# Gate, up and router contract over features 8p+k instead of 128k+p

## The reference

```
x = layer_norm(ALPHA * x + gate1 * (y @ w_out))              # end of the first half
u = x * (1 + scale2) + shift2                                # [512, 1024]
logits  = u @ router_w + router_b                            # 16 experts
# softmax; one group of 4 experts is selected, then 2 experts in it; their scores are normalised
h   = silu(u @ w_gate[e]) * (u @ w_up[e])                    # w_gate, w_up: [16, 1024, 512]
out = sum over the two experts of score * (h @ w_down[e])    # w_down: [16, 512, 1024]
x = layer_norm(ALPHA * x + gate2 * out)
```

## Time and profile before

| | |
|---|---|
| median of 3 runs | 802.93 us (801.92 to 802.96) |
| time of the profiled execution | 803.91 us |
| span of the profiled execution | 802.1 us |
| TensorE matmul busy | 661.9 us, 83% |
| VectorE busy | 346.2 us, 43% |
| ScalarE busy | 249.6 us, 31% |
| GpSimd busy | 120.6 us, 15% |
| moved by DMA | 189.10 MB |
| mean granted TensorE clock | 0.914 of full speed |

### The profile page before, as it was taken

One profiled execution on the slowest core, in us unless ns is written; L12 is line 12 of the kernel. 1 busy time (PEld: TensorE's weight loads), 2 busy tenths in 40 slices (PEclk: granted clock), 3 DMA queues, 4 the chain that ended last, 5 costly groups with the idle time before them and its releaser, 6 DMA issues.

```text
span 802.1 us, 15163 instructions
## 1 busy us (share of the span) xinstructions
PE 661.9 (83%) x5977; PEld 433.7 (54%) x5978; DVE 346.2 (43%) x652; ACT 249.6 (31%) x514; POOL 120.6 (15%) x188
## 2 busy tenths in 40 slices
PE   0799999999897999999987297978997769999800
PEld 0376665777675777777866144534553334555400
DVE  0365553597787856856995500100110000111148
ACT  0344333766454554544012011111111111111144
POOL 0211000200000000000363121211221111222230
PEclk9999999999998999999995589998998798999955
DMA  9999865643112222138849969999999989982152
GB/s 302 373 282 342 273 230 179 222 119 104 55 52 80 80 79 78 57 118 301 339 136 345 349 222 400 400 344 378 330 348 328 378 324 393 335 317 78 42 214 105
DMA packets 109905, 189.10 MB, mean 236 GB/s; under 512 B 4904, under 2 KB 57352, under 8 KB 106800
## 3 DMA queue, kind: packets, MB, share of 16 engines
q1 hardware_dynamic: 96288, 149.05, 53.4%
q0 software_dynamic: 7136, 31.60, 11.0%
q10 hardware_dynamic: 6448, 8.00, 2.8%
HBM read 174.96 MB, written 13.67 MB: 235 GB/s over the span
## 4 chain that ended last, share of the span: by engine, by line
PE 53%; DVE 13%; SPq 13%; DMA 11%; ACT 6%; issue 4%; POOL 0%; DVEq 0%; ACTq 0%; POOLq 0%
PE psum L1431 11%; PE psum L1251 8%; SPq L380 8%; PE psum L1252 8%; PE psum L1253 8%; DMA wu<-in_moe_w_up_dram 7%; PE psum L1442 6%; SPq L385 3%; DMA raw<-in_w_in_dram 3%; PE psum L1217 2%; DVE u L1044 2%; PE psum L1294 1%; SPq L394 1%; PE psum L1306 1%; PE psum L1414 1%
## 5 line engine op out<-in xcount | busy, mean ns | idle before, releaser
L1431 PE MATMUL psum<-wg,xs 128*32 128x256 f32 x1280 | 159.1, 403 | 28.2 <-DMA wu<-in_moe_w_up_dram 24.9
L1431 PE MATMUL psum<-wu,xs 128*32 128x256 f32 x1280 | 158.9, 403 | 0.0
L1251 PE MATMUL psum<-uh,whi 128*128 128x512 f32 x336 | 138.2, 411 | 0.0
L1252 PE MATMUL psum<-ul,whi 128*128 128x512 f32 x336 | 131.7, 392 | 0.0
L1253 PE MATMUL psum<-uh,wlo 128*128 128x512 f32 x336 | 131.6, 392 | 0.0
L1431 PEld LDWEIGHTS psum<-wg,xs 128*32 128x32 f32 x1280 | 75.6, 115 | 84.1 <-DMA wu<-in_moe_w_up_dram 28.9
L1165 DVE TENSOR_TENSOR h_sb<-psum,hsil 64x256 f32<-64x256 f32 x40 | 17.1, 427 | 199.4 <-ACT hsil L759 199.4
L847 DVE TENSOR_TENSOR wlo<-raw,whi 128x1024 fp32r<-128x1024 f32 x42 | 51.4, 1224 | 64.1 <-ACT whi L605 63.9
L1442 PE MATMUL psum<-wd,hT 128*32 128x256 f32 x1280 | 78.2, 385 | 0.4 <-DVE hT L1169 0.4
L1431 PEld LDWEIGHTS psum<-wu,xs 128*32 128x32 f32 x1280 | 74.0, 115 | 3.4 <-issue 3.3
L1251 PEld LDWEIGHTS psum<-uh,whi 128*128 128x128 f32 x336 | 63.5, 189 | 20.5 <-issue 7.1
(11 more groups left out here) (253 smaller groups left out, 862.8 us busy)
## 6 DMA issues: line engine op xcount, KB each, us to landing
wg<-in_moe_w_gate_dram SPq DMA_DIRECT2D x32, 1024.0 KB, 12.3
wu<-in_moe_w_up_dram SPq DMA_DIRECT2D x32, 1024.0 KB, 17.1
wd<-in_moe_w_down_dram SPq DMA_DIRECT2D x32, 1024.0 KB, 14.6
raw<-in_w_in_dram SPq DMA_DIRECT2D x42, 512.0 KB, 4.0
ada<-in_ada_w_dram POOLq DMA_DIRECT2D x16, 1024.0 KB, 6.9
ada<-in_ada_w_dram SPq DMA_DIRECT2D x8, 1024.0 KB, 17.0
y_d<-ysb ACTq DMA_DIRECT2D x40, 128.0 KB
y_d<-zrow POOLq DMA_DIRECT2D x8, 512.0 KB, 6.3
```

The costliest lines, as they stand in the source:

```text
L1251: mmul(bank[s % 2], h[:, k, :], uh[:, k, :], start=(k == 0), stop=False)
L1252: mmul(bank[s % 2], h[:, k, :], ul[:, k, :], start=False, stop=False)
L1431: ins = mmul(psum[32 * g:32 * g + 32, 0, 0:256], xs[:, k % 2, k // 2, :], wgu[slot][g // 2][:, k, (g % 2) * 256:(g % 2) * 256 + 256], star ...
```

## The change

The gate, up and router weights are loaded with the view "(p k)" instead of "(k p)": partition p holds the features 8p to 8p+7, which are adjacent rows in DRAM. A half of k of the gate or up weights is then four adjacent rows of 2 KB on each partition. The down weights keep their order. To match, VectorE writes u2 in the order of (k, p): column 128k+p of a u2 tile holds feature 8p+k. It reads `zt`, `a2r` and `b2r` in their natural order, and writes the result with a step of 128 elements; L1044 reads u2 with the same step. `u2_d`, the gathers and the transposes are the same instructions as before. `x1`, which the second layer norm adds, does not pass through u2.

```diff
-        wg_v = moe_w_gate[0].rearrange("e (k p) f -> e p k f", p=P)
-        wu_v = moe_w_up[0].rearrange("e (k p) f -> e p k f", p=P)
+        wg_v = moe_w_gate[0].rearrange("e (p k) f -> e p k f", p=P)
+        wu_v = moe_w_up[0].rearrange("e (p k) f -> e p k f", p=P)
         wd_v = moe_w_down[0].rearrange("e (k p) n -> e p k n", p=P)
...
-                    pool.dma_start(rw[:, :, :], router_w.rearrange("(k p) e -> p k e", p=P)).then_inc(late_in, 16)
+                    pool.dma_start(rw[:, :, :], router_w.rearrange("(p k) e -> p k e", p=P)).then_inc(late_in, 16)
...
+            def by_k(row):
+                return row[:, :].rearrange("t (p k) -> t p k", k=KT)
+
...
-                v = u2[t % 2][:, :]
-                chain(V.tensor_tensor(v, zt[:, :], a2r[:, :], ALU.mult))
-                V.tensor_tensor(v, v, b2r[:, :], ALU.add).then_inc(S["u2_done"], 1)
+                v = u2[t % 2][:, :].rearrange("t (k p) -> t p k", k=KT)
+                chain(V.tensor_tensor(v, by_k(zt), by_k(a2r), ALU.mult))
+                V.tensor_tensor(v, v, by_k(b2r), ALU.add).then_inc(S["u2_done"], 1)
```

## The result

The changed kernel takes **818.24 us** (median of 4 runs, 816.26 to 819.37) against 802.94 us (801.92 to 803.51) for the kernel before in the same rounds: ratio 1.0177, 95% interval 1.0158 to 1.0195. It is slower by 1.8%, outside the predicted range of 796 to 810 us. The profiled execution has a span of 815.9 us against 802.1.

A forecast was written before the change was run, and what follows sets the result against it. It took DMA to set the time in the expert half up to 663.6 us, then TensorE, with VectorE's u2 stage ahead uncovered. 7.6 - 7.9 = -0.3 us gave 802.6 us on a scale of 802.93, range 796 to 810 us.

The forecast's parts named there:

- The term was +7.6 us: VectorE's u2 lines L1043 and L1044: strided access adds 7.6 us over four tiles, delaying everything behind.
- central bounds of 6.1 and 9.1: u2 cost in us if a stepped write costs as a read: 6.1 if both overlap in L1044, 9.1 if they add.
- the first rival: VectorE's u2 lines: stepped writes are dear, +11.9 us by the skill's 2.50 ns for a small step; chance 0.17.
- the term of -7.9 us: Gate and up loads before 663.6 us: 8 KB pieces load faster than 2 KB ones, saving 7.9 us (middle of 9.1 and 6.7).
- What costs nothing: Router load, first experts' loads, SP's issues, gathers, transposes, matmuls and u2 stores: no cost was added to the sum.
- Stepped writes are dear: L1043 and L1044: u2 costs 15.2 us at the upper bound, sum +7.3 us, 810.2 us; chance 0.17.
- the load rate does not rise: Expert-half loads: no faster rate, so only VectorE's +7.6 us remain, 810.5 us; chance 0.10.
- The stage's own losses shrink too: Expert stage before 663.6 us: losses tied to scattered 2 KB pieces go, 16 us gained, sum -8.4 us, 794.5 us; chance 0.16.

The follow-up runs named there:

- e3: The changed kernel with four `ysb` buffers and four store semaphores instead of two: 813.71 us, ratio 1.012 to the kernel before.
- e15: The changed kernel with each gate and up load cut in two, so pieces are 4 KB in the same feature order: 803.62 us, ratio 0.9996.
- e18: The changed kernel with each gate and up load cut in four, so pieces are 2 KB in the same feature order: 809.27 us, ratio 1.006.
- e1: The changed kernel with gate and up weights loaded in the old order (2 KB pieces), u2 and router edits kept, output wrong: 807.43 us, ratio 1.0044.
- e2: The kernel before with only the gate and up loads in the new order (8 KB pieces), output wrong: 814.03 us, ratio 1.0119.
- e5: The kernel before with gate and up in 4 KB pieces (two adjacent rows), u2 in natural order, transposes reading every second column: 799.56 us, ratio 0.9945.
- e10: e2 with only half of the columns of each y_d store written, in 128 pieces of 512 B: 793.86 us, ratio 0.9876.
- e20: The kernel before with only half of the columns of each y_d store written, in 128 pieces of 512 B: 785.05 us, ratio 0.9765.
- e19: e2 with only half of the partitions of each y_d store written, in 64 pieces of 1 KB: 813.31 us, ratio 1.0112.

## Why the prediction was wrong

**u2: mechanism right, size too high.** The term was +7.6 us with central bounds of 6.1 and 9.1; the two lines measured +5.4 us, and 4.3 us arrived at the first gate/up matmul (3.9 to 6.3 us in the traces of e3, e15, e18 and e1, which have the same edit). A stepped write of 1024 elements costs 0.74 us, 0.72 ns an element, as the stepped reads of the earlier trace rows do. L1047, with a stepped read and write, pays 0.61 us and not twice 0.76. Its wait for GpSimd does not hide more: in the third tile it ends 1.76 us after L531, before 1.09 us, which is 0.67 us. So the steps overlap. The Trainium skill (Vector Engine (DVE) Microarchitecture Reference, section 5.2) gives 1.71 ns a column for a destination that hops 4 KiB at each element, where 1.05 is the price in order. That is 0.66 ns more, against 0.72 here with a hop of 512 bytes: the trace agrees. Its 2.50 ns for a small step was the first rival, and is not seen here.

**Loads: the rate was right, the term had the wrong sign.** 417 GB/s in 505 to 560 us is near the 425 of the earlier trace rows, and all waits for `wu` went. But the term of -7.9 us is in truth **+10 us** (e2). The step that failed is the paragraph "What costs nothing". It says "Gathers share the DMA engines with pieces four times as long" and checks the gathers alone: they have a block to spare, and took 5.9 us instead of 5.6, as was argued. The same sentence holds for the stores of y_d in ScalarE's queue, and no term of the prediction has their time. The trace of before could have given it away. There are only two `ysb` buffers between the down matmuls and the DMA, though ScalarE's waits name no store. And a store took about 4.7 us of a block's 6.1 us, so that only 1.4 us of room were left for longer load pieces.

**Where it tips.** Stores of 4.7 us (2 KB) are hidden in a block of 6.1 us. 6.6 us (4 KB) is just above it, and holds only as long as loads run, so two buffers absorb nearly all of it: e5 gains. 8.6 us (8 KB) is above it by 2.5 us a block: whenever loads run TensorE falls behind, SP then runs dry (the 0.70), and the DMA time that the loads won is lost in pauses, in part of which four engines still work off their arrears (the 0.35). This is also why the last wait was not for a load at 663 us, as forecast.

**The rivals.** None had this mechanism. "Stepped writes are dear" and "the load rate does not rise" gave 810 us by causes that the profile refutes (1962 ns, and 417 GB/s), and the range reached only there. "The stage's own losses shrink too" was wrong in its reason, though e10 and e20 show that such losses exist: they come from the stores.

**Shown, and only argued.** Shown: the length of the load pieces makes stores slow (e15, e18, e5), the number of pieces on an engine counts and not their number in all (e19 against e10 and e2), and it is a rate and not a latency (e3). The Trainium skill (DMA: Bandwidth & Descriptors, "Why a DMA increments its semaphore by 16 and not by 1") says how many engines a DMA uses. It is the largest number up to 16 that divides the slowest dimension of both access patterns, and for a DMA issued from ScalarE they are the lowest-numbered ones. Here the patterns start with 4 (the g of `y_v`) and 128, which gives the 4 that the packets show, and 2 in e19: the trace agrees. That they are the same four each time would also explain the 19 us of e20: 40 stores x 32 pieces x (0.046 - 0.027) us are 24 us less on these four engines, but only 6 if all 16 shared it evenly. The counts by microsecond speak for it, since the arrears stay on four engines from store to store. So do the end packets of the loads. Twelve engines end together and four later in before, in e19 fourteen and two:

```
before, 630.5 to 638.5 us:  12  4  0  12  4  0  12  1
e19,    640.4 to 648.4 us:  14  2  0  16  0  14  2  0
```

The records name no engine, so that it is always the same ones stays an inference. How much of the loss beside 8 KB pieces comes from late stores, and how much from these engines' late share of the loads, no run separates; in after TensorE waits for no load. Not tried: a store whose pattern starts with a multiple of 16 (four stores of 32 partitions, or the rows of a block outermost), which would put 8 pieces on each of 16 engines. As an estimate by the rule of turns, with after's 0.241 + 0.046 us, it would take 8 x 0.287 = 2.3 us.

## What to carry to other kernels

Before making one queue's pieces longer, list every other queue that runs at the same time, and for each the pieces per DMA engine times (its piece + the longer one); compare that with the period at which its buffers come round. Count the 4-byte end packets of a small DMA to see on how many engines it lies: a leading dimension of 4 put all of it on 4 here. Between a length that starves TensorE of weights and one that starves it of free buffers there can be a middle that is faster than both, here 4 KB.

## What the runs showed of the hardware

- Two queues on one DMA engine take turns piece by piece, whatever the pieces' sizes: 32 pieces of 1 KB took 4.7, 6.6 and 8.6 us beside load pieces of 0.106, 0.173 and 0.241 us, and single microseconds show as many load pieces as store pieces on these engines. A store piece of 512 B took 0.027 us instead of 0.046.
- A DMA issued by ScalarE with a leading dimension of 4 had 4 end packets, with 2 it had 2, and the loads had 16. The engines with the stores fell behind the others in the loads, at 569 to 575 us down to a DMA share of 0.35.
- The same 128 KB store issued by GpSimd left 32 packets of 4 KB and 96 of 16 B in the records instead of 128 of 1 KB.
- A pause of 3.2 us in front of 32 matmuls made them 3.25 us instead of 1.86, at a granted clock of 0.57.
